# Sums of squares of the stick-breaking heads: one full-precision matmul, or two in the rounded format over a high and a low part

## The chip, the cores and the metric

The kernel runs on one core of one Trainium2 chip. The metric is the device time of one execution in microseconds. Its engines go by PE (TensorE), ACT (ScalarE), DVE (VectorE), POOL (GpSimd) and SP (SyncE, which here only issues transfers).

## What is computed

Two blocks of a network over 512 positions of width 1024, batch 1, all in float32. The first has banded attention and a convolution; the second has two layers, each a mixer and a squared-ReLU MLP. The change touches only the mixer of the second layer, stick-breaking attention with eight heads of 128, and in it the norm of queries and keys:

```python
def rmsnorm_2(x, g):
    xf = x.astype(jnp.float32)
    y = xf * lax.rsqrt(jnp.mean(xf * xf, axis=-1, keepdims=True) + EPS)
    return (y * g.astype(jnp.float32)).astype(x.dtype)

def mixer_c(n, w_in, gq, gk, w_out):
    q, k, v = _split(n @ w_in, (C_WIDTH, C_WIDTH, C_WIDTH))
    q = rmsnorm_2(q.reshape(bsz, s_len, N_HEADS_C, HEAD_DIM), gq)
    k = rmsnorm_2(k.reshape(bsz, s_len, N_HEADS_C, HEAD_DIM), gk)
    v = v.reshape(bsz, s_len, N_HEADS_C, HEAD_DIM)
    return stick_breaking(q, k, v).reshape(bsz, s_len, C_WIDTH) @ w_out
```

stick_breaking takes the scores z of earlier keys, the reversed running sum rc of log_sigmoid(-z), and the weights exp(log_sigmoid(z) + rc - log_sigmoid(-z)).

## The kernel before, in words

Activations lie transposed: features on the 128 partitions, positions along 512 columns. Weights come as tiles of 1 MB (raw), which SP loads into two slots in turn. A float32 product is made from parts in a rounded format (fp32r): ACT copies a tile into its high part wh (L974, "split" on ACT), DVE subtracts to get the low part wl (L1511, "split" on DVE), and PE makes each 128x128 block of weights with three rounded matmuls, high by high, high by low and low by high (L427 to L429). A block of a head's query or key is 24 such matmuls over 512 columns into bank G0 or G1, in turn; a block of values is 48 over 256 columns.

The stick-breaking mixer goes in four groups (g = 0 to 3) of two heads, and a last one without projections (g = 4) that finishes the heads of group 3. A group has three tiles and six blocks: query and key of its first head (blocks 0, 1), of its second (2, 3), and values (4, 5). Beside them run the scores and weights of the group before, whose heads are called prev and prev+1. The order on each engine is written out by hand, in one function attention_group for each engine, and the engines meet through semaphores alone; each executes its own instructions strictly in the order written.

For each of blocks 0 to 3 the norm goes like this. ACT copies the bank to tmp (L982) and squares it into sq (L989), which has two buffers. PE multiplies sq with a matrix of ones in full float32 (head_stat, L490), so that each partition of bank ST holds the sum over the head's 128 features. This sum waits until the one before it has been applied (st_applied). DVE takes the mean square (L1544), ACT makes the root in three steps (L994 to L996), DVE corrects it (L1536, L1537) and applies it with the gain to a buffer of wide (L1947, x_set), and says so (L1548, st_applied). ACT's copy of block n waits for the root of block n - 2, since tmp has two buffers. The first sum of a group g has the index qk 8 + 4 g; eight earlier ones belong to the first layer.

PE's order in a group: scores(prev), blocks 0 and 1, sum 0, turns(prev), block 2, sum 1, av(prev), scores(prev+1), block 3, sum 2, block 4, turns(prev+1), block 5, sum 3, av(prev+1). "Turns" are ten transpositions of the weights (L517), "av" is their product with the values (L825).

ACT's order: split(0), softplus of the scores of prev (L1268, L1271, L1272), evacuation of block 0 (L982, L989), exponentials of prev (L1281), evacuation of block 1, root 0, copies of the turned weights of prev (L1031), split(1), evacuation of block 2, root 1, softplus of prev+1, evacuation of block 3, split(2), exponentials of prev+1, values of block 4, root 2, turned weights of prev+1, values of block 5, root 3.

DVE's order: split(0), weights(prev), apply(0), split(1), apply(1), output(prev), weights(prev+1), split(2), apply(2), apply(3), output(prev+1). weights() goes through L1979, the running sums L1984 and L1989 in two halves, and each half is followed by an exponential on ACT; the turns need both: the first three transpositions the first half, the fourth also the second. split(k) gives the low part of tile k + 1, so split(2) is that of the next group's first tile. In group 0 there is no prev, and DVE first finishes the layer's norm and copies the position scales out of a bank (L2021). SP loads the next tile into a slot when the low part of the tile in it is made (w_lo).

Of the kernel before, what the change touches and what calls it, by code (L numbers as in the profile page):

```python
# [20 lines left out]
P = 128  # L21
# [13 lines left out]
F = mybir.dt.float32  # L35
R = mybir.dt.float32r
ALU = mybir.AluOpType
ACT = mybir.ActivationFunctionType
# [87 lines left out]
def build(nc, xT, wst, par_d, wg_d, rb_d, small_d, swap_d, tab_d, out):  # L126
    with ExitStack() as ctx:
        def sb(name, shape, dt=F):
            return ctx.enter_context(nc.sbuf_tensor(name, shape, dt))

        def sem(name):
            return ctx.enter_context(nc.semaphore(name))
# [22 lines left out]
        ones = sb("ones", [P, P])  # L155
        ident_r = sb("ident_r", [P, P], R)
        mask_r = sb("mask_r", [P, P], R)
        SbB = sb("SbB", [P, 1280])
        PTB = sb("PTB", [P, 1280])
        cols = sb("cols", [P, 48])  # L160
# [10 lines left out]
        gain2 = sb("gain2", [P, KC])  # L171
        acc = [fb[:, n, :] for n in range(2)]
        far_eps = wide[:, 7, :]
        bfar = cols[:, 16:24]

        loaded, par_in = sem("loaded"), sem("par_in")
# [11 lines left out]
        s_max, s_exp, s_rec, p_ready = sem("s_max"), sem("s_exp"), sem("s_rec"), sem("p_ready")  # L188
        cat_lo, y_lo, hid_sq, hid_hi, hid_lo = (sem(n) for n in ("cat_lo", "y_lo", "hid_sq", "hid_hi", "hid_lo"))
        h_final = sem("h_final")  # L190
        sq_ready, sq_added, sq_used, acc_set = (sem(n) for n in ("sq_ready", "sq_added", "sq_used", "acc_set"))
        masks_set = sem("masks_set")
        r_set, carried = sem("r_set"), sem("carried")
# [210 lines left out]
        def _(pe):  # L404
# [80 lines left out]

            def head_stat(key):
                q = SQ[key]
                pe.wait_ge(st_applied, STAT[key])
                pe.wait_ge(sq_ready, q + 1)
                mm(ps["ST"][:], ones[:], sq[:, q % 2, :], start=True, stop=True).then_inc(sq_used, 1)  # L490
# [472 lines left out]
        def _(act):  # L963
# [20 lines left out]
            def square(key, src):  # L984
                q, m = SQ[key], STAT[key]

                after_norm = [k for k in STAT if STAT[k] == m - 1][0][0] == "norm"
                act.wait_ge(sq_used, m if after_norm else m - 1)
                A(sq[:, q % 2, :], src, ACT.Square).then_inc(sq_ready, 1)  # L989

            def rsqrt(key):
# [510 lines left out]
        def _(dve):  # L1502
# [36 lines left out]
            def mean_square(key, n, eps=None):  # L1539

                dve.wait_ge(sq_used, STAT[key] + 1)
                if eps is None:
                    return ts(tmp[:, 7, :], ps["ST"][:], 1.0 / n, EPS, ALU.mult, ALU.add)
                return stt(out=tmp[:, 7, :], in0=ps["ST"][:], scalar=1.0 / n, in1=eps, op0=ALU.mult, op1=ALU.add)  # L1544

            def applied():

# [385 lines left out]
            def attention_group(name, g, hd, prev, rope, qk0, soft):  # L1933
                st = Step(name, g)

                def apply(n):

                    y = rsqrt(("qk", qk0 + n), P, wide[:, 0, :] if soft else far_eps,
                              lambda: choose(0, 1, 1))
                    if soft:  # L1940
                        gain = par[:, GKA:GKA + 1] if n % 2 else par[:, GQA:GQA + 1]
                        dst, sem_ = tmp[:, 2 + (rope + n) % 2, :], rope_x
                    else:
                        gain = par[:, GKC:GKC + 1] if n % 2 else gq_scaled
                        dst, sem_ = wide[:, 8 + n, :], x_set
                    stands(dve, st, n)
                    stt(out=dst, in0=tmp[:, n % 2, :], scalar=gain, in1=y, op0=ALU.mult, op1=ALU.mult).then_inc(sem_, 1)  # L1947
                    applied()

                def rotated_last(g_):  # L1950

                    r = 4 + 4 * g_
                    rope_add(r, tabA[1], wide[:, 14 + r % 2, :], wide[:, 11, :])

                def rotated(n):
                    if soft:
                        r = rope + n
                        rope_add(r, tabA[1], wide[:, 14 + r % 2, :], wide[:, 8 + n, :])

                def weights(hh, whole=True):  # L1960
                    Sb = MIX_Sb[side(hh)]
                    if soft:
                        for t in range(NT):
                            key = ("score", hh, CBANK[t])
                            w = (t + 1) * P
                            ready(dve, key)
                            ins = stt(out=Sb[:, OFF[t]:OFF[t] + w], in0=bank_of(key)[:, COFF[t]:COFF[t] + w],
                                      scalar=P ** -0.5, in1=idx[:, OFF[t]:OFF[t] + w], op0=ALU.mult, op1=ALU.add)
                            if t:
                                moved_use(ins, key)  # L1970
                        maxima(side(hh))
                        if whole:
                            reciprocals(side(hh), 4 * hh + 4)
                        return

                    for n, banks in enumerate(HALVES):
                        dve.wait_ge(sp_log, 2 * (hh - 12) + n + 1)
                        for b, lo, w in banks:
                            last = stt(out=Sb[:, lo:lo + w], in0=bank_of(("score", hh, b))[:, 0:w], scalar=0.0,  # L1979
                                       in1=Sb[:, lo:lo + w], op0=ALU.max, op1=ALU.add)  # L1980
                        step(last)
                        for t in (3,) if n else (0, 1, 2):
                            back = slice(OFF[t], OFF[t] + (t + 1) * P)
                            last = v.tensor_tensor_scan(suffix[:, back][:, ::-1], extra[:, 0:(t + 1) * P],  # L1984
                                                        Sb[:, back][:, ::-1], 0.0, ALU.mult, ALU.add)
                        step(last)

                        for b, lo, w in banks:
                            moved_use(tt(Sb[:, lo:lo + w], bank_of(("score", hh, b))[:, 0:w], suffix[:, lo:lo + w],  # L1989
                                         ALU.subtract), ("score", hh, b))  # L1990

                def output(hh):
                    key = ("av", hh)
                    c = hh - (8 if soft else 12)
                    ready(dve, key)
                    step(v.tensor_copy(oh[:, c, :], bank_of(key)[:]))
                    release(tt(ol[:, c, :], bank_of(key)[:], oh[:, c, :].bitcast(F), ALU.subtract), key)  # L1997
# [25 lines left out]
                    weights(prev)  # L2023
                if soft and g:
                    rotated_last(g)
                apply(0)
                if not soft:
                    split(st, 1)
                apply(1)
# [1 line left out]
                choose(0, 0, 1)  # L2031
                if prev is not None:
                    output(prev)
                    weights(prev + 1)
                rotated(1)
                if soft:
                    apply(2)
# [14 lines left out]

            dve.wait_ge(tables_in, 64)
            step(v.tensor_copy(ident_r[:], ident))
            v.tensor_copy(mask_r[:], small[:, C_SN:C_SN + P]).then_inc(masks_set, 1)
            for g in range(2):
                attention_group("dsa", g, 8 + 2 * g, 6 + 2 * g if g else None, 5 + 4 * g, 4 * g, True)
# [152 lines left out]
```

## Time and profile before

| | before |
|---|---|
| median of 3 runs | 1691.37 us (1690.5 to 1692.4) |
| the profiled execution | 1692.81 us |
| its span, first to last instruction | 1690.9 us |
| mean granted TensorE clock | 0.989 |
| PE busy | 1638.1 us, 97% |
| DVE busy | 882.2 us, 52% |
| ACT busy | 603.3 us, 36% |
| POOL busy | 263.8 us, 16% |
| DMA | 146.56 MB, 87 GB/s |
| chain that ended last, share on PE | 88% |
| one weight tile, issue to landing | 4.8 us |

Busy time counts an engine's own instructions. A matmul's end is modelled, so the rows of PE are read by their starts. In the stick-breaking mixer group 0 has its first sum at 1100 us and its last at 1126; groups 1 to 3 begin at 1127, 1175 and 1224 us; the last group begins at 1272 us.

### The profile page before, as it was taken

The numbers are of one execution on the slowest core, as the hardware profiler recorded it, in microseconds if no ns is written. First come the engines' busy times: TensorE is split into PE (matmuls) and PEld (weight loads), VectorE is DVE, ScalarE is ACT, GpSimd is POOL, SyncE is SP. The second block draws the span as 40 slices with busy tenths as digits, with TensorE's granted clock in tenths as the row PEclk, the third lists the DMA queues.
The fourth block names the chain that finished last, engine by engine and source line by source line (L and its number), as shares of the span: only waits on it lengthen the run. The fifth ranks groups of instructions, "written<-read, shape, count | busy, mean of one in ns | idle before, by whom it ended". The sixth has DMA issues, their size and how long they took to land.

```text
span 1690.9 us, 20231 instructions
## 1 busy us (share of the span) xinstructions
PE 1638.1 (97%) x7650; PEld 1328.9 (79%) x7650; DVE 882.2 (52%) x1166; ACT 603.3 (36%) x801; POOL 263.8 (16%) x288
## 2 busy tenths in 40 slices
PE   7999999999998899899999999999998999999999
PEld 7888787787667677688888888888885888888887
DVE  7335555556669785554343434456675543434343
ACT  6323333233334345332222222457665321212121
POOL 0001111023315154221010101200000210101010
PEclk9999999999889999999999999999999999999999
DMA  5221222222111212122222222221120222222222
GB/s 205 100 100 75 76 98 99 81 94 92 58 50 51 66 50 76 50 93 107 81 100 93 99 99 100 100 75 54 72 75 26 100 100 100 96 102 80 98 99 100
DMA packets 25012, 146.56 MB, mean 87 GB/s; under 512 B 3680, under 2 KB 4976, under 8 KB 8304
## 3 DMA queue, kind: packets, MB, share of 16 engines
q1 hardware_dynamic: 24944, 145.62, 24.5%
q8 instruction: 47, 0.77, 0.2%
q14 instruction: 21, 0.17, 0.0%
HBM read 143.52 MB, written 2.10 MB: 86 GB/s over the span
## 4 chain that ended last, share of the span: by engine, by line
PE 88%; DVE 7%; ACT 2%; issue 2%; POOL 1%; DMA 0%; SPq 0%; DVEq 0%; ACTq 0%; POOLq 0%
PE ps_G L427 27%; PE ps_G L428 26%; PE ps_G L429 26%; PE ps_ST L490 1%; PE ps_C L500 1%; DVE wide L1842 1%; DVE top L1838 1%; PE ps_AV L825 1%; PE ps_C L517 1%; PE ps_SX L687 1%; PE ps_C L605 1%; PE ps_AV L632 1%; PE ps_C L825 1%; POOL wl L1444 0%; DVE tmp L1537 0%
## 5 line engine op out<-in xcount | busy, mean ns | idle before, releaser
L427 PE MATMUL ps_G<-nh,wh 128*128 128x512 f32 x1056 | 413.5, 392 | 9.8 <-DVE nl L1997 6.5
L429 PE MATMUL ps_G<-nh,wl 128*128 128x512 f32 x1056 | 411.0, 389 | 0.0
L428 PE MATMUL ps_G<-nl,wh 128*128 128x512 f32 x1056 | 410.9, 389 | 0.0
L974 ACT ACTIVATE wh<-raw 128x2048 fp32r<-128x2048 f32 x129 | 246.2, 1909 | 328.4 <-PE ps_G L429 314.0
L427 PE MATMUL ps_G<-ch,wh 128*128 128x512 f32 x880 | 356.0, 405 | 6.8 <-POOL wl L1444 4.1
L428 PE MATMUL ps_G<-cl,wh 128*128 128x512 f32 x880 | 345.7, 393 | 0.0
L429 PE MATMUL ps_G<-ch,wl 128*128 128x512 f32 x880 | 345.4, 392 | 0.0
L1511 DVE TENSOR_TENSOR wl<-raw,wh 128x2048 fp32r<-128x2048 f32 x118 | 272.1, 2306 | 131.7 <-ACT wh L974 126.8
L427 PEld LDWEIGHTS ps_G<-nh,wh 128*128 128x128 f32 x1056 | 198.4, 188 | 57.3 <-DVE nl L1997 6.9
L429 PEld LDWEIGHTS ps_G<-nh,wl 128*128 128x128 f32 x1056 | 198.2, 188 | 41.5
L428 PEld LDWEIGHTS ps_G<-nl,wh 128*128 128x128 f32 x1056 | 198.3, 188 | 40.7 <-issue 0.2
L427 PEld LDWEIGHTS ps_G<-ch,wh 128*128 128x128 f32 x880 | 167.3, 190 | 50.6 <-issue 8.1
L428 PEld LDWEIGHTS ps_G<-cl,wh 128*128 128x128 f32 x880 | 167.5, 190 | 38.3 <-issue 4.6
L429 PEld LDWEIGHTS ps_G<-ch,wl 128*128 128x128 f32 x880 | 167.0, 190 | 35.6
L1485 POOL TENSOR_TENSOR tmp<-tmp 128x512 f32<-128x512 f32 x64 | 66.7, 1042 | 540.5 <-DVE tmp L2069 540.5
L2078 DVE TENSOR_TENSOR h<-h,ps_G 128x512 f32<-128x512 f32 x64 | 44.0, 687 | 168.2 <-PE ps_G L429 168.2
L1349 ACT ACTIVATE nh<-tmp 128x512 fp32r<-128x512 f32 x64 | 40.5, 633 | 247.8 <-DVE tmp L2069 247.8
L2069 DVE SCALAR_TENSOR_TENSOR tmp<-ps_G,tmp 128x512 f32<-128x512 f32 x64 | 44.1, 689 | 91.1 <-PE ps_G L429 91.0
L1444 POOL TENSOR_TENSOR wl<-raw,wh 128x256 fp32r<-128x256 f32 x96 | 72.7, 797 | 75.8 <-ACT wh L974 75.7
L2073 DVE TENSOR_TENSOR nl<-tmp,nh 128x512 fp32r<-128x512 f32 x64 | 44.3, 692 | 76.1 <-POOL tmp L1485 76.1
L1383 POOL TENSOR_TENSOR fb<-fb,sq 128x512 f32<-128x512 f32 x40 | 54.5, 1369 | 155.7 <-ACT sq L1016 150.4
L427 PE MATMUL ps_G<-wh,ch 128*128 128x256 f32 x256 | 76.3, 298 | 1.7 <-DVE tmp L1881 1.7
(306 smaller groups left out, 1680.3 us busy)
## 6 DMA issues: line engine op xcount, KB each, us to landing
raw<-wst SPq DMA_DIRECT2D x130, 1024.0 KB, 4.8
raw<-wst SPq DMA_DIRECT2D x4, 512.0 KB, 6.7
h<-xT SPq DMA_DIRECT2D x8, 256.0 KB, 6.1
outT<-h SPq DMA_DIRECT2D x8, 256.0 KB, 2.0
tabs<-rb_d SPq DMA_DIRECT2D x1, 1024.0 KB, 10.4
tabs<-tab_d SPq DMA_DIRECT2D x1, 1024.0 KB, 5.1
tabs<-tab_d SPq DMA_DIRECT2D x1, 512.0 KB, 3.8
small<-small_d SPq DMA_DIRECT2D x1, 192.0 KB, 8.4
```

The lines of the kernel that those rows point to most:

```text
L427: mm(o, ah, bh, start=first, stop=False)
L428: mm(o, ah, bl, start=False, stop=False)
L429: return mm(o, al, bh, start=False, stop=last)
L974: A(wh[s][:], raw[s][:], ACT.Copy).then_inc(w_hi, 1)
L1349: A(oh[:, k, :], tmp[:, k % 2, :], ACT.Square).then_inc(hid_hi, 1)
L1383: g.tensor_tensor(acc[a], acc[a], sq[:, (SQ[("norm", n)] + b) % 2, :], ALU.add).then_inc(sq_added, 1)
L1444: ins = g.tensor_tensor(wl[s][:, c, :], raw[s][:, c, :], wh[s][:, c, :].bitcast(F), ALU.subtract)
L1485: g.tensor_tensor(tmp[:, 2 + k % 2, :], tmp[:, k % 2, :], tmp[:, k % 2, :], ALU.mult).then_inc(hid_sq, 1)
L1511: v.tensor_tensor(wl[s][:], raw[s][:], wh[s][:].bitcast(F), ALU.subtract).then_inc(w_lo, 1)
L2069: moved_block(stt(out=tmp[:, k % 2, :], in0=ready_block(st, k), scalar=0.0, in1=tmp[:, 5, :], op0=ALU.max, op1=ALU.mult), st, k)
L2073: tt(ol[:, k, :], tmp[:, 2 + k % 2, :], oh[:, k, :].bitcast(F), ALU.subtract).then_inc(hid_lo, 1)
L2078: moved_block(tt(h[:, k - 8, :], h[:, k - 8, :], ready_block(st, k), ALU.add), st, k)
```

## The change

The sixteen sums of the stick-breaking heads (qk 8 to 23) are made another way. ACT squares the block twice: first into a high part in the rounded format, then, as before, in full precision into sq. DVE subtracts the one from the other and gets a low part (square_low, semaphore sq_low). PE multiplies a rounded matrix of ones with the high and then the low part into one bank. The parts have two buffers, in oh and ol. The sums of even index go to bank ST and those of odd index to bank SX, so a sum waits for the last but one to be applied, in place of the last. On DVE the low parts are made ahead of a root: 0 and 1 ahead of apply(0), 2 behind apply(0) and ahead of split(1), 3 behind weights(prev+1) and ahead of split(2). The rounded ones are copied once, at the start of the first layer's attention.

```diff
+        ones_r = sb("ones_r", [P, P], R)
...
+        def sum_bank(key):
+
+            return ps["SX"] if key[0] == "qk" and key[1] >= 8 and key[1] % 2 else ps["ST"]
+
+        sq_parts = [(oh[:, 6 + n, :], ol[:, 6 + n, :]) for n in range(2)]
...
             def head_stat(key):
                 q = SQ[key]
+                if key[0] == "qk" and key[1] >= 8:
+                    n = key[1] - 8
+                    pe.wait_ge(st_applied, STAT[key] - (1 if n else 0))
+                    pe.wait_ge(sq_low, n + 1)
+                    o = sum_bank(key)
+                    mm(o[:], ones_r[:], sq_parts[n % 2][0], start=True, stop=False)
+                    mm(o[:], ones_r[:], sq_parts[n % 2][1], start=False, stop=True).then_inc(sq_used, 1)
+                    return
                 pe.wait_ge(st_applied, STAT[key])
                 pe.wait_ge(sq_ready, q + 1)
                 mm(ps["ST"][:], ones[:], sq[:, q % 2, :], start=True, stop=True).then_inc(sq_used, 1)
...
                 act.wait_ge(sq_used, m if after_norm else m - 1)
+                if key[0] == "qk" and key[1] >= 8:
+                    A(sq_parts[(key[1] - 8) % 2][0], src, ACT.Square)
                 A(sq[:, q % 2, :], src, ACT.Square).then_inc(sq_ready, 1)
...
-                return stt(out=tmp[:, 7, :], in0=ps["ST"][:], scalar=1.0 / n, in1=eps, op0=ALU.mult, op1=ALU.add)
+                return stt(out=tmp[:, 7, :], in0=sum_bank(key)[:], scalar=1.0 / n, in1=eps, op0=ALU.mult, op1=ALU.add)
...
+                def square_low(*blocks_):
+                    for n in blocks_ if not soft else ():
+                        hi, lo = sq_parts[n % 2]
+                        q = SQ[("qk", qk0 + n)]
+                        dve.wait_ge(sq_ready, q + 1)
+                        tt(lo, sq[:, q % 2, :], hi.bitcast(F), ALU.subtract).then_inc(sq_low, 1)
+
...
+                square_low(0, 1)
                 apply(0)
+                square_low(2)
                 if not soft:
                     split(st, 1)
                 apply(1)
...
                 if prev is not None:
                     output(prev)
+                if prev is not None:
                     weights(prev + 1)
+                square_low(3)
                 rotated(1)
...
             step(v.tensor_copy(ident_r[:], ident))
+            step(v.tensor_copy(ones_r[:], ones[:]))
```

## Rows read from the trace of the kernel before

**Rows 1.** Windows of the stage: us, busy us (count) of PE, PEld, DVE, ACT, POOL; clock; DMA

```profile
1190.00:1250.00 60.00, 60.00 (x316) 48.24 (x313) 40.33 (x56) 42.42 (x66) 0.00 (x0) 1.00 0.19 65
```

**Rows 2.** Timeline of PE, groups 0 to 2: start us, us, instruction

```profile
1100.04 1.10 PE L490 MATMUL ps_ST<-sq,ones 128*128 128x512 f32 x2
...
1140.23 1.02 PE L490 MATMUL ps_ST<-sq,ones 128*128 128x512 f32 x2
...
1188.65 0.39 PE L429 MATMUL ps_G<-ch,wl 128*128 128x512 f32 x1
...
1188.88 1.02 PE L490 MATMUL ps_ST<-sq,ones 128*128 128x512 f32 x2
...
1189.74 1.25 PE L517 MATMUL ps_C<-small,Sb 128*128 128x128 f32 x10
...
1213.99 1.25 PE L517 MATMUL ps_C<-small,Sb 128*128 128x128 f32 x10
...
1215.01 0.36 PE L427 MATMUL ps_G<-wh,ch 128*128 128x256 f32 x1
...
1220.83 1.02 PE L490 MATMUL ps_ST<-sq,ones 128*128 128x512 f32 x2
```

**Rows 3.** Timeline of ACT, group 2: start us, us, instruction

```profile
1189.20 0.58 ACT L982 ACTIVATE tmp<-ps_G 128x512 f32<-128x512 f32 x1
...
1189.81 0.64 ACT L989 ACTIVATE sq<-tmp 128x512 f32<-128x512 f32 x1
...
1193.82 1.93 ACT L974 ACTIVATE wh<-raw 128x2048 fp32r<-128x2048 f32 x1
...
1210.62 1.35 ACT L1281 ACTIVATE Sb<-Sb 128x768 f32<-128x768 f32 x2
```

**Rows 4.** Timeline of DVE, groups 0 to 2, idle time ahead in brackets

```profile
1100.21 0.16 DVE L2021 COPY cols<-ps_AV 128x4 f32<-128x4 f32 x1 [1.70 <-PE ps_AV L483]
...
1126.92 0.69 DVE L1544 SCALAR_TENSOR_TENSOR tmp<-ps_ST,wide 128x512 f32<-128x512 f32 x1 [1.62 <-PE ps_ST L490]
...
1140.12 0.69 DVE L1989 TENSOR_TENSOR Sb<-ps_C,wide 128x512 f32<-128x512 f32 x1
...
1173.40 0.69 DVE L1544 SCALAR_TENSOR_TENSOR tmp<-ps_ST,wide 128x512 f32<-128x512 f32 x1 [2.71 <-PE ps_ST L490]
...
1187.93 0.69 DVE L1989 TENSOR_TENSOR Sb<-ps_C,wide 128x512 f32<-128x512 f32 x1
...
1190.01 0.69 DVE L1544 SCALAR_TENSOR_TENSOR tmp<-ps_ST,wide 128x512 f32<-128x512 f32 x1 [1.38 <-PE ps_ST L490]
...
1195.78 2.29 DVE L1511 TENSOR_TENSOR wl<-raw,wh 128x2048 fp32r<-128x2048 f32 x1 [0.79 <-ACT wh L974]
...
1197.99 0.68 DVE L1544 SCALAR_TENSOR_TENSOR tmp<-ps_ST,wide 128x512 f32<-128x512 f32 x1
...
1210.31 0.69 DVE L1989 TENSOR_TENSOR Sb<-ps_C,wide 128x512 f32<-128x512 f32 x1
...
1221.89 0.69 DVE L1544 SCALAR_TENSOR_TENSOR tmp<-ps_ST,wide 128x512 f32<-128x512 f32 x1 [2.71 <-PE ps_ST L490]
```

**Rows 5.** The page's groups with a rounded result: busy us, mean ns | idle before

```profile
L1349 ACT ACTIVATE nh<-tmp 128x512 fp32r<-128x512 f32 x64 | 40.5, 633 | 247.8 <-DVE tmp L2069 247.8
...
L2073 DVE TENSOR_TENSOR nl<-tmp,nh 128x512 fp32r<-128x512 f32 x64 | 44.3, 692 | 76.1 <-POOL tmp L1485 76.1
```

**Rows 6.** Timeline of PE, two waits elsewhere, their length in brackets

```profile
534.65 0.39 PE L427 MATMUL ps_G<-wh,ch 128*128 128x256 f32 x1 [1.73 <-DVE tmp L1881]
...
1276.83 0.46 PE L500 MATMUL ps_ST<-wide 128*128 128x128 f32 x2 [1.77 <-DVE nl L1997]
```

**Rows 7.** Windows around those two waits, columns as in rows 1

```profile
537.00:540.00 3.00, 3.00 (x27) 3.00 (x26) 2.59 (x3) 1.04 (x3) 3.00 (x4) 1.00 0.00 0
...
1276.00:1280.00 4.00, 3.17 (x10) 2.10 (x11) 3.93 (x7) 3.10 (x7) 0.00 (x0) 0.73 0.00 0
...
1280.00:1284.00 4.00, 4.00 (x16) 2.90 (x15) 3.83 (x7) 3.90 (x6) 0.00 (x0) 0.85 0.00 0
```

More of the change, by code:

```diff
@@ L190, in build @@
         h_final = sem("h_final")
+        sq_low = sem("sq_low")
         sq_ready, sq_added, sq_used, acc_set = (sem(n) for n in ("sq_ready", "sq_added", "sq_used", "acc_set"))
```

## The prediction, made before the changed kernel had run

> **What bounds the kernel now.** Read first the page's busy shares (PE, TensorE, at 97%, in the table above), then the windows by stage: in the middle of the stick-breaking stage PE is busy for all 60 of 60 us at clock 1.00, while VectorE (DVE) is busy 40 and ScalarE (ACT) 42 [rows 1]. So PE time removed here is worth its full length, as long as PE is not made to wait. Then the timelines of the three engines over group 2, side by side [rows 2 to 4], for what stands behind what in each queue: DVE and ACT have idle time, but it is spent waiting for each other in one long chain. What matters is the slack between that chain and the PE instructions that need its result.
>
> I hold each group against one mark, the fourth mean square (L1544 of block 3, "the exit"). After it come the root, the next group's split(0) and weights(prev), always in the same order; what delays the exit delays the next group.
>
> **What PE saves.** One full-precision sum takes 0.86 us of PE (1188.88 to 1189.74), and one rounded 128x512 matmul 0.23 (1188.65 to 1188.88) [rows 2]. Two of those are 0.46 where 0.86 was, so 0.40 less, and for 16 sums 6.4 us. I take that the rounded pair behaves like its neighbours. Bounds: at worst the pair costs the old 0.86 (no saving), at best nothing better than 0.40 each. The wait for the previous sum to be applied also goes (once, in group 0); it is replaced below.
>
> **What is added on ACT and DVE.** 16 squares on ACT with a rounded result: 0.63 each alone [rows 5], but 0.54 of queue since the next instruction overlaps its end. 16 subtractions on DVE, 0.69 each [rows 5], some 0.60 in the queue. That is 9 and 10 us in engines with room; the place is what counts. The copy of ones into ones_r is one small DVE instruction in the first attention stage: it takes at most the 0.2 us or so of a quarter of a 128x512 pass, there DVE has gaps, I take 0, and 0.3 if they don't cover it. DMA: SP's weight loads wait for the DVE splits, so they start up to 5 us later; a load lands in 4.8 us (table above) and each slot has over ten more until ACT splits it, I take 0. POOL has no work in this stage. The bank choice needs no new wait: the second bank is asked for by nobody until the last group's scores, which already wait for the last root.
>
> **Group 2 step by step, its entry held at the old time.**
> (a) low(0) stands behind weights(prev), whose last L1989 starts at 1187.93 and ends at 1188.62 [rows 4]. low(0) ends at about 1189.35. PE would be there at 1188.8, so it waits some 0.6 us; the sum then ends at 1189.85, against 1189.74 before [rows 2]: the first sum of a group gives nothing.
> (b) low(1) stands ahead of apply(0) and needs block 1's squares. ACT copies block 1 at 1189.20, its first square starts at 1189.81 [rows 3], the second at 1190.35 and ends at 1190.98. low(1) holds DVE to 1191.6, where L1544 started at 1190.01 [rows 4]. So the first root starts 1.6 us late, and ACT's split(1), queued behind it, goes from 1193.82 [rows 3] to 1195.4.
> (c) low(2) stands ahead of DVE's split(1), and needs the squares of block 2, which ACT makes only after that split: copy 1197.2 (after some 1.8 of split), squares from 1197.8 and 1198.4, done 1199.0, low(2) to 1199.65. Then the split of 2.21 (1195.78 to 1197.99 before), then L1544 of block 1 at 1201.85. It was at 1197.99 [rows 4]: 3.86 us late. Before, DVE did this split as soon as ACT's half was there; now it waits for block 2's whole evacuation. This is the step that decides.
> (d) Everything behind it on DVE, output(prev) and weights(prev+1), comes 3.86 late: the last L1989 from 1210.31 [rows 4] to 1214.17, and with it the exponential on ACT, which now ends at 1215.5.
> (e) PE, saving twice 0.40 by then, comes to turns(prev+1) at 1213.3 instead of 1213.99 [rows 2], and needs that exponential for its fourth transposition at 1213.6. It waits 1.9 us. Before, the slack was 2.35 (exponentials from 1210.62 for 1.35 us [rows 3], needed 0.3 after 1213.99).
> (f) From there PE needs 0.7 for the remaining turns, 5.8 for block 5 (1215.01 to 1220.83 [rows 2]), 0.46 for the sum, 0.3 to the reader: exit at 1222.8, against 1221.89 [rows 4]. **Group 2 costs 0.9 us instead of saving 1.6**, and group 3, the same pattern, costs 0.9.
>
> **Groups 0 and 1.** In group 0, DVE must first copy the scales (L2021, 1100.21 [rows 4]) and then do low(0) to 1101.1, where PE was ready at 1100.04 [rows 2]: 1.1 us of waiting. The same (b) and (c) push the later roots by up to 4 us, but no turns hang on them and PE keeps its saving; only the last root, at 1127.7 instead of 1126.92 [rows 4], is late: 0.8. In group 1 PE comes early (1138.9 for the sum that started at 1140.23 [rows 2]) and the chain late: the last L1989 of weights(prev) from 1140.12 [rows 4] to 1140.9, low(0) to 1142.35. So PE waits 3.5 us. The root there had stood only 0.5 behind L1989 instead of 1.4, so low(1) costs 2.4 instead of 1.6, and the exit, formerly 1173.40 [rows 4], comes at 1175.9: 1.7 more.
> Sum without the clock: 0.8 + 1.7 + 0.9 + 0.9 = **4.3 us later**. The last group's chain hangs on the last exit, through the apply that PE already waits for (its wait of 1.77 us [rows 6] stays), so nothing is won back there; behind it PE is full again.
>
> **The clock.** The row of 1276.83 shows a wait of 1.77 us after dense work [rows 6], and the granted clock then fell to 0.73 and 0.85 in two windows of 4 us [rows 7], means of stretches at 1.2 and at 2.4 GHz: 0.27 x 4 + 0.15 x 4 = 1.7 us lost. A wait of 1.73 at 534.65 was followed by no fall [rows 6, 7]. Of two waits of nearly the same length one was followed by a fall: one of 1.9 may be or not, one of 3.5 I take to be. I count a fall in group 1 at its first sum; PE loses 1.7, of which 1.1 reaches the chain through block 2's later end. Of the two waits of 1.9 in groups 2 and 3 I count one, 1.7 in full, since block 5 and the last sum stand right behind it (bounds 0 and 3.4, the last with perhaps 1.7 more in group 1). The Trainium skill ("TensorE: Matmul & The Clock Gate", section on HAM oscillation) speaks of long pauses as what re-throttles PE; by that the waits of 1.9 would be free and the forecast would be lower by 1.7. The row of 1276.83 speaks against it.
> **Sum:** 4.3 + 1.1 + 1.7 = 7.1. The profiled execution took 1692.81 us (span 1690.9), 1.4 above the median of 1691.37; against its own time that is 1699.9, against the median **1698.5**.
>
> **Rivals.**
> A, the forecast: the chain of (b) to (f), with one or more falls of the clock, 1697 to 1703. Chance 0.55.
> B, the same chain and the clock stays up: + 4.3, 1695.7. For it, the 1.73 us wait without a fall; against it, the 3.5 us wait in group 1. 0.18.
> C, the chain has more slack than worked out (the low parts start some tenths earlier, DVE and ACT overlap better), so the waits at the turns are short: from -3 to +3, 1688.5 to 1694.5. 0.12.
> D, the other side: the low parts and squares fall into idle time. DVE idles 2.7 us before L1544 of block 3 [rows 4], and some 2 before each step behind ACT's root. It is decided at one place, the second exponential ahead of turns(prev+1): if (b) and (c) delay it by less than the 2.35 us of slack, PE never waits for it and keeps all 16 x 0.40: 1685.0. Against it, (c) alone holds a 2.2 us split behind an evacuation. 0.12.
> E, not what it says: the rounded pair costs the old 0.86. Then nothing is saved on PE, but the waits swallow most of it; exit later by 0.4 per group, 1.6 more in all, up to 1705 with further falls. 0.03.
>
> **How the numbers follow.** A measurement of this kernel can tell about 0.2%, 3.4 us, from no change. Slower: A, E and 0.14 of B (its 4.3 is close to the bound): 0.72. Same: the rest of B and C: 0.16. Faster: D, 0.12. The range leaves out D and the end of C below, and above three falls and E: 1692.5 to 1703.5.
>
> **What would show it.** The sum pairs on PE about 0.40 us shorter each. L1544 of block 0 later behind L1989 by 1.6, L1544 of block 1 by nearly 4 behind its old place in the group, and DVE idle ahead of low(1) and low(2), released by ACT's square. PE idle ahead of the fourth transposition of turns(prev+1), some 2 us in groups 1 to 3, released by the exponential, and 3 to 4 us ahead of group 1's first sum, released by the low part. Granted clock below 1.00 in windows between 1140 and 1225, where before it was 1.00 throughout. The stages before 1090 and behind the last group unchanged. Wrong is the forecast if PE shows no wait at the turns (then D), or if the waits stand there and the clock doesn't fall (then B).

## The result, and the profile after

The changed kernel takes **1697.92 us** (median of 6 runs, 1693.25 to 1699.92) against 1691.7 us for the kernel before (6 runs, 1690.5 to 1692.79). The ratio is 1.0035, with a 95% interval from 1.0024 to 1.0045: slower by 6 us. The forecast was 1698.5. The six runs of the changed kernel spread over 6.7 us, so that a median within 0.6 us of the forecast is partly luck. The profiled execution took 1699.92 us, span 1698.1, 7.2 us longer than the span before. The page (span; PE's busy time; the chain that ended last, by engine):

```profile
span 1698.1 us, 20264 instructions
...
PE 1634.6 (96%) x7650; PEld 1329.9 (78%) x7650; DVE 893.3 (53%) x1183; ACT 612.3 (36%) x817; POOL 264.1 (16%) x288
...
PE 81%; DVE 12%; ACT 4%; issue 2%; POOL 1%; DMA 0%; SPq 0%; DVEq 0%; ACTq 0%; POOLq 0%
```

PE is busy for 3.5 us less than before and waits for more; in the chain that ended last PE has 81% instead of 88%, DVE 12% instead of 7%. Since each group's fourth mean square marks its end, the whole change can be read in five intervals, each the difference of two starts of that instruction, the first from the norm's mean square and the last to the end of the span:

| us | group 0 | group 1 | group 2 | group 3 | from there to the end |
|---|---|---|---|---|---|
| before | 33.19 | 46.48 | 48.49 | 48.49 | 420.52 |
| after | 34.15 | 50.34 | 49.44 | 49.43 | 420.45 |
| difference | +0.96 | +3.86 | +0.95 | +0.94 | -0.07 |

That is 6.6 of the 7.2 us. The other 0.6 lies ahead of the stage (the norm's mean square at 1094.29 instead of 1093.73), where nothing was changed but the copy of the ones; in the second profiled execution of the same kernel it stands at 1092.2, so it is scatter.

The starts behind the table, and DVE's timeline in group 2 (start us, us, instruction, idle time in brackets), answer to [rows 4]. L1959 is the low part, L1562 the mean square (ST or SX), L2014 the old L1989, L1529 the split:

```profile
1128.44 0.68 DVE L1562 SCALAR_TENSOR_TENSOR tmp<-ps_SX,wide 128x512 f32<-128x512 f32 x1
...
1178.78 0.69 DVE L1562 SCALAR_TENSOR_TENSOR tmp<-ps_SX,wide 128x512 f32<-128x512 f32 x1
...
1193.32 0.69 DVE L2014 TENSOR_TENSOR Sb<-ps_C,wide 128x512 f32<-128x512 f32 x1
1194.04 0.69 DVE L1959 TENSOR_TENSOR nl<-sq,nh 128x512 fp32r<-128x512 f32 x1
1196.38 0.69 DVE L1959 TENSOR_TENSOR nl<-sq,nh 128x512 fp32r<-128x512 f32 x1 [1.65 <-ACT sq L1007]
1196.99 0.68 DVE L1562 SCALAR_TENSOR_TENSOR tmp<-ps_ST,wide 128x512 f32<-128x512 f32 x1
...
1204.42 0.69 DVE L1959 TENSOR_TENSOR nl<-sq,nh 128x512 fp32r<-128x512 f32 x1 [2.45 <-ACT sq L1007]
1205.03 2.28 DVE L1529 TENSOR_TENSOR wl<-raw,wh 128x2048 fp32r<-128x2048 f32 x1
1207.23 0.68 DVE L1562 SCALAR_TENSOR_TENSOR tmp<-ps_SX,wide 128x512 f32<-128x512 f32 x1
...
1219.57 0.69 DVE L2014 TENSOR_TENSOR Sb<-ps_C,wide 128x512 f32<-128x512 f32 x1
...
1228.22 0.69 DVE L1562 SCALAR_TENSOR_TENSOR tmp<-ps_SX,wide 128x512 f32<-128x512 f32 x1
```

The mean square of block 0 starts 3.67 us behind the last L2014 (1193.32 to 1196.99), 2.08 before; the second one 13.91 behind it, 10.06 before. Both low parts are preceded by idle time, 1.65 and 2.45 us, which ends with ACT's second square. ACT in the same stretch, against [rows 3]: L1006 and L1007 are the two squares, L990 is the split and L998 the copy of block 2.

```profile
1195.19 0.63 ACT L1006 ACTIVATE nh<-tmp 128x512 fp32r<-128x512 f32 x1
1195.73 0.62 ACT L1007 ACTIVATE sq<-tmp 128x512 f32<-128x512 f32 x1
...
1200.80 1.93 ACT L990 ACTIVATE wh<-raw 128x2048 fp32r<-128x2048 f32 x1
1202.61 0.60 ACT L998 ACTIVATE tmp<-ps_G 128x512 f32<-128x512 f32 x1
...
1203.77 0.62 ACT L1007 ACTIVATE sq<-tmp 128x512 f32<-128x512 f32 x1
```

The copy of block 2 starts as soon as the split lets it, and the low part (1204.42) as soon as the second square behind it is done. PE, against [rows 2]:

```profile
1143.21 0.77 PE L501 MATMUL ps_ST<-nh,ones_r 128*128 128x512 f32 x1 [3.35 <-DVE nl L1959]
...
1194.88 0.47 PE L501 MATMUL ps_ST<-nh,ones_r 128*128 128x512 f32 x1 [0.47 <-DVE nl L1959]
1195.19 0.39 PE L502 MATMUL ps_ST<-nl,ones_r 128*128 128x512 f32 x1
1195.42 1.25 PE L533 MATMUL ps_C<-small,Sb 128*128 128x128 f32 x10
...
1220.54 1.42 PE L533 MATMUL ps_C<-small,Sb 128*128 128x128 f32 x10 [1.49 <-DVE Sb L2014]
1221.71 0.36 PE L435 MATMUL ps_G<-wh,ch 128*128 128x256 f32 x1
...
1227.55 0.40 PE L501 MATMUL ps_SX<-nh,ones_r 128*128 128x512 f32 x1
1227.78 0.40 PE L502 MATMUL ps_SX<-nl,ones_r 128*128 128x512 f32 x1
1228.02 2.32 PE L841 MATMUL ps_AV<-PT,wide 128*128 128x512 f32 x8
```

A pair of rounded matmuls takes 0.47 us (1227.55 to 1228.02) where the full sum took 0.86. The ten transpositions of turns(prev+1) begin at 1220.54, and block 5 at 1221.71. What PE waited for in the whole stage (us in total, times, longest):

```profile
PE ps_ST L501 <- DVE nl L1959: 5.4, 4, 3.3
PE ps_C L533 <- DVE Sb L2014: 4.0, 3, 1.5
PE ps_ST L516 <- DVE nl L2022: 1.8, 1, 1.8
PE ps_ST L533 <- ACT SbB L1299: 1.6, 1, 1.6
```

Before, the first two rows weren't there; the last two, in the last group, were, at 1.8 and 1.6 us. In the windows (columns as in [rows 1]) the stage's middle is no longer full, and the clock has fallen once in groups 0 to 3:

```profile
1190.00:1250.00 60.00, 57.57 (x310) 47.65 (x309) 42.90 (x62) 41.80 (x68) 0.00 (x0) 1.00 0.18 63
...
1140.00:1144.00 4.00, 0.79 (x2) 0.72 (x3) 2.96 (x4) 2.10 (x4) 0.00 (x0) 0.74 0.00 0
1144.00:1148.00 4.00, 4.00 (x15) 3.45 (x14) 1.29 (x2) 2.58 (x6) 0.00 (x0) 0.50 0.00 0
1148.00:1152.00 4.00, 4.00 (x17) 3.28 (x16) 2.20 (x4) 3.04 (x4) 0.00 (x0) 0.91 0.00 0
...
1220.00:1224.00 4.00, 3.46 (x29) 3.34 (x30) 3.75 (x4) 1.54 (x4) 0.00 (x0) 1.00 0.00 0
```

The fall follows the wait of 3.35 us ahead of group 1's sum: 0.26 + 0.50 + 0.09 of 4 us each, 3.4 us of full clock lost, against 1.7 in [rows 7]. After group 2's wait at the turns the clock stays at 1.00.

### The profile page after: what moved, and what is told of

Read it like the earlier page. It is cut to its first block, busy times and chain, and to the rows that moved or that the text cites. A ratio compares the mean times of both kernels' runs of the same rounds, so it can differ in the third digit from the quotient of the medians.

```text
span 1698.1 us, 20264 instructions
## 1 busy us (share of the span) xinstructions
PE 1634.6 (96%) x7650; PEld 1329.9 (78%) x7650; DVE 893.3 (53%) x1183; ACT 612.3 (36%) x817; POOL 264.1 (16%) x288
## 4 chain that ended last, share of the span: by engine, by line
PE 81%; DVE 12%; ACT 4%; issue 2%; POOL 1%; DMA 0%; SPq 0%; DVEq 0%; ACTq 0%; POOLq 0%
PE ps_G L435 25%; PE ps_G L437 25%; PE ps_G L436 25%; DVE wl L1529 1%; DVE wide L2009 1%; DVE wide L1860 1%; DVE top L1856 1%; PE ps_C L533 1%; DVE tmp L1554 1%; DVE Sb L2014 1%; DVE tmp L1555 1%; PE ps_SX L703 1%; DVE Sb L2004 1%; PE ps_C L621 1%; PE ps_AV L648 1%
## 5 line engine op out<-in xcount | busy, mean ns | idle before, releaser
L990 ACT ACTIVATE wh<-raw 128x2048 fp32r<-128x2048 f32 x129 | 246.4, 1910 | 328.1 <-PE ps_G L437 313.7
L1529 DVE TENSOR_TENSOR wl<-raw,wh 128x2048 fp32r<-128x2048 f32 x118 | 272.0, 2305 | 127.8 <-ACT wh L990 123.0
L1503 POOL TENSOR_TENSOR tmp<-tmp 128x512 f32<-128x512 f32 x64 | 66.7, 1042 | 540.5 <-DVE tmp L2099 540.5
```

Of the source, the lines that this page charges most:

```text
L990: A(wh[s][:], raw[s][:], ACT.Copy).then_inc(w_hi, 1)
L1503: g.tensor_tensor(tmp[:, 2 + k % 2, :], tmp[:, k % 2, :], tmp[:, k % 2, :], ALU.mult).then_inc(hid_sq, 1)
L1529: v.tensor_tensor(wl[s][:], raw[s][:], wh[s][:].bitcast(F), ALU.subtract).then_inc(w_lo, 1)
```

## The experiments

The theory was the order: a low part stands in DVE's queue ahead of a root or a split, waits there for ACT, and holds up the chain until PE has to wait. The rival was the load: 16 squares and 16 subtractions cost what they cost wherever they stand. A second question was what the clock has in it. The ratios are to runs of the kernel before that were made beside them (medians 1691.15, 1691.41 and 1691.41 us). The intervals of all of them:

| us | median | ratio to before, 95% interval | group 0 | 1 | 2 | 3 |
|---|---|---|---|---|---|---|
| changed kernel again | 1698.79 | 1.0047 (1.0033 to 1.0061) | 34.15 | 50.35 | 49.42 | 49.42 |
| low 1 behind root 0 | 1694.99 | 1.0026 (1.0016 to 1.0036) | 34.16 | 47.74 | 49.06 | 49.03 |
| low 2 behind split 1 | 1687.58 | 0.9982 (0.9973 to 0.9992) | 32.10 | 46.41 | 47.75 | 47.74 |
| both behind | 1689.01 | 0.9990 (0.9981 to 1.0000) | 34.42 | 46.30 | 47.60 | 47.61 |
| low 0 between halves too | 1689.23 | 0.9987 (0.9978 to 0.9996) | 34.40 | 46.23 | 47.58 | 47.57 |
| best order on DVE | 1687.80 | 0.9980 (0.9971 to 0.9989) | 31.51 | 46.24 | 47.58 | 47.58 |
| PE's part alone | 1683.03 | 0.9958 (0.9944 to 0.9971) | 30.87 | 45.35 | 46.94 | 46.94 |
| low parts on POOL | 1683.55 | 0.9955 (0.9941 to 0.9968) | 30.87 | 45.32 | 46.94 | 46.94 |
| full sums kept | 1697.34 | 1.0038 (1.0023 to 1.0052) | 34.57 | 48.50 | 49.83 | 49.83 |
| group 1's wait filled | 1695.21 | 1.0024 (1.0015 to 1.0032) | 34.15 | 48.09 | 49.42 | 49.43 |

Intervals repeat to some hundredths between executions; medians scatter by more, for a reason given at the end.

### Low part 1 behind the first root

```diff
-                square_low(0, 1)
+                square_low(0)
                 apply(0)
-                square_low(2)
+                square_low(1, 2)
```

> Low part 1 moved behind apply(0) (low 0, apply 0, low 1 and 2, split 1); low part 2 still ahead of split(1). Theory (order: the low parts hold up the chain of roots and splits): the first root of a group starts 1.6 us earlier, but low(2) still waits for the evacuation of block 2, so the second mean square gains only some 0.6 us in each of groups 1 to 3; about 1696, 2 below the changed kernel, and PE still waits 1 us or more at turns(prev+1). Rival (load: the 16 squares and 16 subtractions cost time wherever they stand, or slow their neighbours): no difference to the changed kernel, 1698.

Measured: 1694.99 us. Groups 2 and 3 got shorter by 0.4 each. The second mean square of group 2 starts 13.56 us behind the last L2014 instead of 13.91, a gain of 0.35 where 0.6 was expected; the low part that waits for block 2 still sits ahead of the split. Group 1 gained 2.6, most of it because the clock did not fall in this execution, after a wait only a little shorter. PE's timeline of this kernel at that wait:

```profile
1139.72 0.47 PE L501 MATMUL ps_ST<-nh,ones_r 128*128 128x512 f32 x1 [2.77 <-DVE nl L1959]
```

and the windows around it:

```profile
1136.00:1140.00 4.00, 1.23 (x6) 0.74 (x5) 3.44 (x5) 1.96 (x3) 0.00 (x0) 1.00 0.08 35
1140.00:1144.00 4.00, 4.00 (x24) 3.40 (x23) 1.47 (x3) 3.90 (x8) 0.00 (x0) 1.00 0.00 0
```

So this half of the change's order is the small one, as the theory has it, and the clock's fall is not certain after such a wait.

### Low part 2 behind the second split

```diff
                 apply(0)
-                square_low(2)
                 if not soft:
                     split(st, 1)
+                square_low(2)
                 apply(1)
```

> Low part 2 moved behind split(1) and ahead of apply(1); low part 1 still ahead of apply(0). Theory (order): the second mean square comes 1.7 us earlier than in the changed kernel, PE's wait at turns(prev+1) falls from 1.5 us to 0.3 or less, and the first sum of group 1 is waited for less long; about 1691.5, between 1689.5 and 1693. Rival (load): 1698.

Measured: 1687.58 us, **10 us less for one line moved by two**, and faster than the kernel before. The step itself came out as expected: the second mean square of group 2 starts 12.24 us behind the last L2014 instead of 13.91, 1.67 earlier, and PE has no wait at the turns. The time lies below the expected range. The intervals are shorter than in the changed kernel by 2.05, 3.93, 1.69 and 1.69 us; the expectation speaks neither of group 0 nor of the clock, and in group 1, whose first sum now waits 1.3 us, no clock was lost in this execution. Against the kernel before they are shorter by 1.09, 0.07, 0.74 and 0.75. PE's wait ahead of the first sums, which stays (us in total, times, longest):

```profile
PE ps_ST L501 <- DVE nl L1959: 3.3, 4, 1.3
```

The same kernel once more, to compare the last two experiments with:

> Low part 2 moved behind split(1) alone, once more, beside the two on the same chip: 1687.6 again, 3.5 below the kernel before.

Measured: 1687.68 us.

### Both moved

```diff
-                square_low(0, 1)
+                square_low(0)
                 apply(0)
-                square_low(2)
+                square_low(1)
                 if not soft:
                     split(st, 1)
                 apply(1)
+                square_low(2)
```

> Both moved: low 0, apply 0, low 1, split 1, apply 1, low 2. Theory (order): the chain is back at its old place but for 0.8 us at weights(prev+1), PE has no wait at turns(prev+1) and only some 0.6 us at a group's first sum, so each group keeps 3 of its 4 savings of 0.40 us: about 1688.4, between 1687 and 1690, faster than the kernel before. Rival (load): 1698.

Measured: 1689.01 us, inside the expected range, but not better than the one move. Groups 1 to 3 are shorter by 0.1 to 0.15 each, and group 0 is longer by 2.3: with low 2 behind apply(1) PE waits 1.54 us for it in group 0, where it has no turns and scores of a head before to do, and 0.33 us for low 1. PE's timeline of this kernel, group 0's third sum:

```profile
1115.34 0.47 PE L501 MATMUL ps_ST<-nh,ones_r 128*128 128x512 f32 x1 [1.54 <-DVE nl L1959]
```

### Low part 0 between the halves of weights(prev)

```diff
+                        if n == 0:
+                            between()
...
-                    weights(prev)
+                    weights(prev, between=lambda: square_low(0))
...
+                if prev is None:
+                    square_low(0)
                 apply(0)
+                square_low(1)
                 if not soft:
                     split(st, 1)
                 apply(1)
+                square_low(2)
```

> As the kernel with both low parts moved behind (low 0, apply 0, low 1, split 1, apply 1, low 2), and low part 0 moved further, between the two halves of weights(prev), so that a group's first sum need not wait for it. Theory (order): PE no longer waits for low(0), but the second half and its exponential come 0.6 us later, and the fourth transposition of turns(prev) waits for that instead: 0.1 to 0.3 us a group better than without, about 1688. Rival: the first sum gains its full 0.40 too and more, 1686.5 or less.

Measured: 1689.23 us; intervals shorter by 0.02 to 0.07 than with both moved. That is less than the 0.1 to 0.3 expected. In group 1 the wait of 1.27 us ahead of the first sum is gone, and one of 0.79 stands ahead of turns(prev) instead; in groups 2 and 3 the ten transpositions, which come next, are recorded with 1.45 us instead of 1.25. So at this place low part 0 costs nearly the same ahead of the second half's last instruction as behind it.

### The best order on DVE

```diff
                 applied()
+                square_low(0)
                 ready(dve, ("rt", 4))
...
                 apply(0)
+                square_low(1)
                 split(st, 1)
+                if g == 0:
+                    square_low(2)
                 apply(1)
+                if g:
+                    square_low(2)
```

with low part 0 of groups 1 to 3 between the halves, as in the last one.

> All low parts still on VectorE, each where its input is there and nothing waits behind it: in group 0 low 0 ahead of the copy of the position scales (L2046), apply 0, low 1, split 1, low 2, apply 1; in groups 1 to 3 low 0 between the halves of weights(prev), apply 0, low 1, split 1, apply 1, low 2. Theory (order): group 0 loses its wait of 1.07 us and its exit comes some 31.2 us after the norm's mean square (32.1 with low 2 behind split 1, 34.4 with both moved), groups 1 to 3 as measured with low 0 between the halves, 46.2, 47.6 and 47.6; about 1686.4. Rival (the order is used up, the rest is ScalarE's second square): 1687.5 or more.

Measured: 1687.80 us beside 1687.68 for low part 2 behind split 1. By the intervals it is 1.1 us better (31.51, 46.24, 47.58, 47.58 against 32.10, 46.43, 47.76, 47.75 in that execution), by the medians not at all. The medians don't decide it; a microsecond is below what ten runs can tell here. The rival's number, 1687.5 or more, came true, but its reason, ACT's second square, is ruled out by the kernel with the low parts on POOL below, which keeps that square.

### TensorE's part alone

```diff
-                    pe.wait_ge(sq_low, n + 1)
+                    pe.wait_ge(sq_ready, q + 1)
...
-                    mm(o[:], ones_r[:], sq_parts[n % 2][1], start=False, stop=True).then_inc(sq_used, 1)
+                    mm(o[:], ones_r[:], sq_parts[n % 2][0], start=False, stop=True).then_inc(sq_used, 1)
...
-                    A(sq_parts[(key[1] - 8) % 2][0], src, ACT.Square)
+                    A(sq_parts[(key[1] - 8) % 2][0], src, ACT.Square).then_inc(sq_ready, 1)
+                    return
...
-                    for n in blocks_ if not soft else ():
+                    for n in ():
```

> TensorE's part alone: the two rounded matmuls both take the high part, the full square on ScalarE and all low parts on VectorE are left out (the low part of the squares is not summed). Theory (order): the PE side of the change is worth its full 16 x 0.40 us when nothing is put into the chain: 1685.3, between 1684 and 1687. Rival (the rounded pair costs more than its neighbours show, or the end of the stage hangs on something else): over 1689.

Measured: 1683.03 us. This kernel leaves out the low part of the squares and ACT's second square, so it prices PE's work and doesn't make the whole sum. The four intervals are shorter than before by 2.32, 1.13, 1.55 and 1.55, together **6.55 us**, where 16 x 0.40 is 6.4 and the wait for the first sum to be applied was 0.4. The median gained 8.1, 2 more than expected. In the profiled execution the clock did not fall in the last group, which makes the rest 418.74 us instead of 420.5, as in five others of the table's kernels; whether that holds for the other five runs isn't shown.

### The full sums kept, with all that was added

```diff
-                    mm(o[:], ones_r[:], sq_parts[n % 2][0], start=True, stop=False)
-                    mm(o[:], ones_r[:], sq_parts[n % 2][1], start=False, stop=True).then_inc(sq_used, 1)
+                    mm(o[:], ones[:], sq[:, q % 2, :], start=True, stop=True).then_inc(sq_used, 1)
```

> The changed kernel with all its squares, low parts and waits, but each sum made again by one full-precision matmul over sq (the parts are made and not used). Theory (order): PE has waits ahead of the exponentials that swallow what it saves, so taking the saving away costs only the last sum of each group, 0.4 x 3 = 1.2 us, and the long wait of group 1 shrinks by some 1.4 us, with perhaps no fall of the clock (up to 3 us less): 1696 to 1699. Rival (PE's saving of 6.4 us counts in full, and the added work costs 13 us): 1704.

Measured: 1697.34 us. Each group is 0.4 us longer than in the changed kernel with the clock up: group 0 by 0.42, groups 2 and 3 by 0.41, and group 1 by 0.41 against the 48.09 us of the next experiment. That is one sum of the four. Against the changed kernel itself group 1 is 1.8 shorter, since the wait is shorter and the clock stays up in this execution. PE's timeline at group 1's first sum:

```profile
1140.62 1.10 PE L501 MATMUL ps_ST<-sq,ones 128*128 128x512 f32 x2 [2.17 <-DVE nl L1958]
```

So in the order of the change only the last sum's saving of a group reaches its exit, some 1.6 of the 6.4 us; the waits swallow the rest. The rival's 1704 is out.

### The wait of group 1 filled

```diff
+                    if n == 4:
+                        for _ in range(14):
+                            mm(o[:], ones_r[:], mh[:, 0, :], start=True, stop=True)
                     pe.wait_ge(sq_low, n + 1)
```

> The changed kernel with 14 more rounded matmuls (3.2 us, their result overwritten) ahead of the wait for low part 0 in group 1 alone, where PE idles 3.35 us. Theory (clock: this wait makes the granted clock fall, 3.4 us of work lost in the profiled run): clock 1.00 from 1140 to 1156, the sum of group 1 starts at the same time, and the time falls to 1695.3, with single runs no more than 2 us apart. Rival (the fall has nothing to do with the wait, or costs nothing on the path): 1697.9 and the same spread of 6 us.

Measured: 1695.21 us, beside 1698.79 us for the changed kernel on the same chip; the granted clock stays at 1.00. The windows of this kernel, and behind them PE's timeline:

```profile
1136.00:1140.00 4.00, 4.00 (x19) 3.25 (x18) 3.83 (x6) 1.41 (x3) 0.00 (x0) 1.00 0.34 139
1140.00:1144.00 4.00, 4.00 (x23) 3.15 (x22) 1.79 (x3) 2.61 (x5) 0.00 (x0) 1.00 0.00 0
1144.00:1148.00 4.00, 4.00 (x19) 3.29 (x19) 2.20 (x4) 3.94 (x7) 0.00 (x0) 1.00 0.00 0
```

```profile
1137.14 3.43 PE L502 MATMUL ps_ST<-ch,ones_r 128*128 128x512 f32 x14
1140.55 0.50 PE L504 MATMUL ps_ST<-nh,ones_r 128*128 128x512 f32 x1
```

The sum starts 48.8 us behind the norm's mean square (1140.55 less 1091.73), and 48.9 in the changed kernel, so the filling did not move it. Group 1 takes 48.09 us instead of 50.34: the fall of the clock cost **2.25 us**, and 1.6 us (48.09 less 46.48) remain for the chain. The runs still spread over 4.2 us (1692.61 to 1696.78), less than the 7.9 of the changed kernel beside it but more than the 2 expected, so part of the spread has another source.

The changed kernel beside it:

> The changed kernel again, beside the next ones on the same chip. 1697.9 us, single runs from 1693 to 1700; that spread comes from the clock after the wait in group 1, if the theory of the clock holds, and then goes with the mean granted clock of each run.

Measured: 1698.79 us (1695.45 to 1703.37), with a wait of 3.34 us and the same fall in group 1. The single runs went with their mean granted clock, as expected: 1695.45 us at 0.991, 1703.37 us at 0.985. That the fall in group 1 makes this whole spread isn't shown, since 4.2 of the 7.9 us are left with the wait filled.

### The low parts on POOL

```diff
+            for n in range(16):
+                hi, lo = sq_parts[n % 2]
+                q = SQ[("qk", 8 + n)]
+                pool.wait_ge(sq_ready, q + 1)
+                g.tensor_tensor(lo, sq[:, q % 2, :], hi.bitcast(F), ALU.subtract).then_inc(sq_low, 1)
             out_squares("outc", 5)
...
-                square_low(0, 1)
                 apply(0)
-                square_low(2)
...
-                square_low(3)
```

> The 16 low parts on GpSimd, which has no work in this stage; VectorE's order is that of the kernel before, ScalarE's two squares stay. Theory (order: only what stands in the DVE queue ahead of a root or a split costs): the time comes near TensorE's part alone, which has neither low parts nor a second square: 1683.5 to 1685. Rival (load: GpSimd beside VectorE slows both, as a mean of 1042 ns for its 128x512 against 692 hints): VectorE's 128x512 instructions over 0.69 us, and 1686 or more.

Measured: **1683.55 us**, 0.9955 (0.9941 to 0.9968) of the kernel before, 14 us below the changed kernel. The intervals are those of PE's part alone, to 0.03 us: ACT's second square costs nothing, and neither does the subtraction once it is out of DVE's queue. PE's waits in the stage are the old ones of the last group and 0.2 us:

```profile
PE ps_G L435 <- DVE nl L2020: 3.1, 2, 1.6
PE ps_ST L516 <- DVE nl L2020: 1.8, 1, 1.8
...
PE ps_C L533 <- DVE Sb L2012: 0.2, 1, 0.2
```

The groups of instructions in the stage (busy us, mean ns | idle before): DVE's splits keep their old pace, and POOL, at 1319 ns, has plenty of idle time.

```profile
L1534 DVE TENSOR_TENSOR wl<-raw,wh 128x2048 fp32r<-128x2048 f32 x11 | 25.2, 2288 | 6.1 <-ACT wh L990 6.0
...
L1519 POOL TENSOR_TENSOR nl<-sq,nh 128x512 fp32r<-128x512 f32 x16 | 21.1, 1319 | 141.3 <-ACT sq L1007 141.3
...
```

Of the rival, that POOL beside DVE slows both, a part is true all the same. DVE's running sums over 128x512 (L2007, L1984 before) took 1.22 or 1.23 us each in the kernel before. In this one three of them, all in weights(prev+1), ran beside one of POOL's subtractions for over half a microsecond and took 1.67, 1.92 and 1.92 us. Group 2 of this kernel, and the same running sum before (start us, us, instruction):

```profile
1203.97 1.31 POOL L1519 TENSOR_TENSOR nl<-sq,nh 128x512 fp32r<-128x512 f32 x1 [9.38 <-ACT sq L1007]
1204.43 1.92 DVE L2007 TENSOR_TENSOR_SCAN wide<-extra,Sb 128x512 f32<-128x512 f32 x1
...
1209.05 1.23 DVE L1984 TENSOR_TENSOR_SCAN wide<-extra,Sb 128x512 f32<-128x512 f32 x1
```

That is 1.8 us more for DVE in all, ahead of turns(prev+1), where PE comes late enough not to wait for it: the intervals show none of it.

## Why the prediction was right, step by step

**What PE saves** was right: 0.39 for each sum (0.86 to 0.47), 6.55 us in all with nothing added to DVE's queue, of which some 0.4 is the wait for a sum to be applied.

**(a)** A group's first sum waits for low(0): forecast 0.6, measured 0.47 in group 2. PE starts the sum 0.15 us behind the end of low(0) (1194.73 to 1194.88), which the forecast left out. **(b)** The first root: forecast 1.6 us late, measured 1.59 (3.67 less 2.08). **(c)** The second: forecast 3.86, measured 3.85 (13.91 less 10.06). That this is the step that decides was tested: with low 2 out of the way the time fell by 10 us, with low 1 out of the way by 3. In the profiled executions 2.25 us of either are the clock in group 1. **(d), (e)** PE waits at turns(prev+1): forecast 1.9, measured 1.49 ahead of the first transposition and another 0.15 inside the ten (1.17 us instead of 1.02). The chain itself was forecast to the hundredth: the last L2014 starts at 1219.57, which is 1214.18 with the 5.39 us taken off by which this group begins later, forecast 1214.17. PE came later than forecast, by the same measure at 1213.66 instead of 1213.3, and this makes the wait shorter. The instruction was wrong: I had PE wait for the second exponential at the fourth transposition. It waits ahead of the first, for DVE's last L2014, since the turns also need the score bank that L2014 gives back; that the 0.15 us are the wait for the exponential is likely from the order, not shown. **(f)** The exit of groups 2 and 3: forecast 0.9 each, measured 0.95 and 0.94.

**Group 0**: forecast 0.8, measured 0.96. **Group 1**: forecast a wait of 3.5 us and 1.7 us without the clock; measured 3.35, and 1.6 with the wait filled. The sum without the clock was 4.3 and came to 4.5 (0.96, 1.61, 0.95, 0.94).

**The clock** was near in total, 2.25 us for a forecast of 2.8, by luck: two errors cancel. Forecast were 1.1 in group 1 and 1.7 in one of the later groups; measured were 2.25 in group 1, twice the forecast, and nothing in groups 2 and 3, where the waits were 1.5 instead of 1.9. The term that was too small is the fall in group 1: 3.4 us of full clock lost instead of the 1.7 of [rows 7], of which 2.25 reached the exit. The Trainium skill ("TensorE: Matmul & The Clock Gate", section on HAM oscillation) names long pauses as the cause, and the stage's longest wait, 3.35 and 3.34 us, was followed by a fall in both profiled executions, which agrees, as was one of 4.12 us ahead of the matmul at 544.79 in the kernel before (granted clock 0.50 from 544 to 548). But a wait of 1.8 us in the last group was followed by a fall in some executions of nearly the same instructions and by none in others, and one of 2.77 us by none, so neither the length of the wait alone nor my one row could tell; the falls after 1.8 us are not what that section would have one expect.

**Rivals.** B, the chain with a steady clock, is what the filled wait made: 1695.21, forecast 1695.7. C, more slack in the chain, is out by the 1.59 and 3.85 us of (b) and (c). D, which needed less than 2.35 us of delay ahead of turns(prev+1), is what moving low part 2 made: the wait at the turns went away. It kept only part of the saving, though (1687.58, not 1685.0): the first sums still wait. E is out, by the 0.47 us of a pair.

## What to carry to other kernels

Cheap work added to an engine with idle time isn't free if it stands, with a wait of its own, ahead of something that others need: here a subtraction of 0.69 us ahead of a split, once in each of four groups, made a 10 us difference by its place alone, of which 2.25 us came by the clock. Work out for each added instruction what it waits for and what is queued behind it, put it behind the last thing that somebody needs now, or give it to an engine whose queue is empty. Then a slower engine can be the better one: POOL took 1.3 us for each subtraction, DVE 0.69, and that kernel was the fastest of those that make the whole sum.

## What was not expected of the hardware

**POOL beside DVE.** The Trainium skill ("GPSIMD Engine Reference", section 1, Specifications) says that GpSimd shares its SBUF interfaces with VectorE and that instructions of VectorE with two SBUF inputs contend with it, and (section 3) that VectorE stays the engine for elementwise work. The trace agrees with the first: the running sums, with two SBUF inputs, took 0.45, 0.69 and 0.69 us longer where they ran into a subtraction for 0.57, 0.85 and 0.84 us. L2002, which reads one of its inputs from a bank of PSUM, took the same 0.69 us wholly beside one (1181.19, subtraction from 1180.78 to 1182.08). The 11 splits of DVE, which have two SBUF inputs too, took 25.2 us in all as before, but only three subtractions ran beside one, for its last 0.43, 0.18 and 0.18 us; the first of them took 1.57 us, where most took 1.30:

```profile
1144.48 2.29 DVE L1534 TENSOR_TENSOR wl<-raw,wh 128x2048 fp32r<-128x2048 f32 x1 [0.78 <-ACT wh L990]
1146.34 1.57 POOL L1519 TENSOR_TENSOR nl<-sq,nh 128x512 fp32r<-128x512 f32 x1 [5.42 <-ACT sq L1007]
```

So the kernel is fast since the two meet seldom, and where DVE has slack; what a full overlap costs isn't shown. The second did not hold for the kernel's time, 1683.55 us against 1687.8 with the best order on DVE. POOL's subtraction took 1319 ns on average, against 1042 for L1485 in the MLPs of the kernel before, whose two inputs are one tensor and whose result is not rounded; which of these makes the difference isn't shown.

**The clock's falls vary from run to run.** The last group's wait of 1.8 us was followed by a loss of 1.7 us in six profiled executions (the kernel before, the changed one twice, three variants) and by none in the seven others, although the instructions there are the same; the time from the last exit to the end is 420.5 us with the fall and 418.8 without. Before the stage, between 440 and 640 us, the windows of the profiled executions show between 11.9 and 17.2 us of lost clock, and the stage begins between 1090.8 and 1094.8 us, with code that is the same in all of them but for the copy of the ones. This goes with a spread of 2 to 8 us in the times of one kernel, the kernel before included (1687.38 to 1693.19 in one job), and it is why differences of a microsecond were read from the intervals and not from the medians. Why a wait of 1.8 us was followed by a fall in some executions and not in others, and one of 2.77 us by none, stays open.
